# Stick-breaking attention: value products in groups of four units, in every other round, with a ring of ten turned tiles

## The reference

```python
def block(args):                       # one block of 128 queries
    z = q @ k.T * scale
    strict = key_pos < q_pos
    log_1mb = where(strict, log_sigmoid(-z), 0)
    after = reverse_cumsum(log_1mb) - log_1mb
    a = where(strict, exp(log_sigmoid(z) + after), 0)
    return a @ v
```

## Time and profile before

| | us |
|---|---|
| median of three runs | 2894.77 |
| the profiled execution, its own time | 2895.18 |
| its span | 2893.4 |
| attention stage, first scores to last output copy | 592.2 to 1050.5 |
| PE busy in the span | 2622.1 (91%) |
| DVE, ACT, POOL busy in the span | 1493.9, 1316.4, 629.1 |

### The profile page before, as it was taken

How to read it: one execution, slowest core, us unless ns; L and a number is a source line. 1 busy time by engine, 2 the same in 40 slices (tenths; PEclk the granted TensorE clock), 3 DMA queues, 4 the chain that set the end, 5 groups by cost and what they waited for, 6 DMA issues and landing times. The chain is left out here.

```text
span 2893.4 us, 46489 instructions
## 1 busy us (share of the span) xinstructions
PE 2622.1 (91%) x14633; PEld 2095.4 (72%) x14635; DVE 1493.9 (52%) x1975; ACT 1316.4 (45%) x2332; POOL 629.1 (22%) x697
## 2 busy tenths in 40 slices
PE   7999689979999979978999999949999999999991
PEld 6888578856667657757678888737777788888880
DVE  4222245578888862220433333265788855555643
ACT  4222233278989961100322222124777755555642
POOL 0000011157777730000000000031222211112223
PEclk9999899989999989989999999959999999999995
DMA  4333411242021022232312221143999966666856
GB/s 167 94 91 94 135 61 59 62 89 67 16 67 49 2 88 98 101 141 104 114 53 78 87 80 59 66 170 118 372 372 367 355 217 210 208 213 219 282 152 249
DMA packets 203097, 406.93 MB, mean 141 GB/s; under 512 B 26096, under 2 KB 67568, under 8 KB 202992
## 3 DMA queue, kind: packets, MB, share of 16 engines
q1 hardware_dynamic: 186576, 363.04, 36.1%
q0 software_dynamic: 13968, 33.59, 5.0%
q10 hardware_dynamic: 2448, 8.91, 0.8%
HBM read 339.39 MB, written 83.36 MB: 146 GB/s over the span
## 5 line engine op out<-in xcount | busy, mean ns | idle before, releaser
L746 POOL TENSOR_TENSOR stick_weight<-stick_weight,stick_left 128x512 f32<-128x512 f32 (+3 forms) x320 | 327.9, 1038 | 127.0 <-DVE stick_left L874 122.6
L1625 DVE TENSOR_TENSOR moe_w_lo<-moe_w_lo_raw,moe_w_hi (+1 forms) x256 | 297.7, 1220 | 57.6 <-ACT moe_w_hi L1621 51.8
L1621 ACT CAST moe_w_hi<-moe_w_lo_raw (+1 forms) x256 | 255.2, 1054 | 39.3 <-DMA moe_w_lo_raw<-in_w 29.3
L874 DVE TENSOR_TENSOR_SCAN stick_left<-stick_z_ps,stick_left,stick_any_row 128x512 f32<-128x512 f32 x192 | 240.3, 1276 | 35.4 <-ACT stick_z_ps L837 35.1
L835 ACT ACTIVATE stick_weight<-stick_z_ps 128x512 f32<-128x512 f32 (+3 forms) x320 | 173.6, 542 | 32.7 <-PE stick_z_ps L784 21.1
L797 PE MATMUL stick_t_ps<-all_ident,stick_weight 128*128 128x128 f32 x1088 | 165.2, 281 | 18.8 <-ACT stick_weight_t L844 9.2
L58 PE MATMUL exp_g_ps<-moe_w_hi,exp_x_hi 128*128 x376 | 154.7, 411 | 22.0 <-DVE moe_w_lo L1625 11.1
L837 ACT ACTIVATE stick_z_ps<-stick_z_ps 128x512 f32<-128x512 f32 (+3 forms) x320 | 165.7, 518 | 10.4
L797 PEld LDWEIGHTS stick_t_ps<-all_ident,stick_weight 128*128 128x128 f32 x1088 | 116.1, 141 | 69.7 <-issue 45.6
L58 PE MATMUL qkv_z_ps<-qkv_w_hi,qkv_h_hi 128*128 128x512 f32 x384 | 157.5, 410 | 4.0 <-DVE qkv_h_lo L238 4.0
L58 PE MATMUL exp_y_ps<-moe_w_hi,exp_h_hi 128*128 128x512 f32 x376 | 153.5, 408 | 2.3 <-DVE exp_h_lo L2054 2.3
(11 more groups left out here) (287 smaller groups left out, 5934.9 us busy)
## 6 DMA issues: line engine op xcount, KB each, us to landing
moe_w_lo_raw<-in_w SPq DMA_DIRECT2D x512, 256.0 KB
moe_w_lo_raw<-in_w SPq DMA_DIRECT2D x128, 512.0 KB
qkv_xs<-in_x SPq DMA_DIRECT2D x16, 512.0 KB, 4.7
qt_scratch<-qkv_q_t SPq DMA_DIRECT2D x16, 512.0 KB, 3.2
kt_scratch<-qkv_k_t SPq DMA_DIRECT2D x16, 512.0 KB, 3.5
gmlp_xs<-in_x SPq DMA_DIRECT2D x16, 512.0 KB, 3.7
mix_q<-qt_scratch SPq DMA_DIRECT2D x32, 256.0 KB
out_xs<-in_x SPq DMA_DIRECT2D x16, 512.0 KB, 3.4
```

The source lines that it names most:

```text
L746: nc.gpsimd.tensor_tensor(taken, taken, after, ALU.mult).then_inc(weight_done, 1)
L874: nc.vector.tensor_tensor_scan(row[:, c * BANK:c * BANK + keys][:, ::-1], back, any_row[:, 0:keys], start, ALU.mult, ALU.bypass).then_inc( ...
L1621: nc.scalar.copy(self.w13_hi[:, self.w13_at(e, i)], self.w13_raw[:, self.w13_at(e, i)]).then_inc(self.w13_cut, 1)
L1625: ops.tensor_tensor(self.w13_lo[:, self.w13_at(e, i)], self.w13_raw[:, self.w13_at(e, i)], as_f32(self.w13_hi[:, self.w13_at(e, i)]), ALU. ...
```

## The change

PE's round of even index (n a multiple of 4) now holds the value products of four units, n-8 to n-5; the other rounds hold none. The ring `weight_t` has ten slots where it had six. `put_out` stands two steps later in ACT's list (OUT_AT 9 where it was 7).

```diff
-    SLOTS, W_SLOTS, T_SLOTS, LEFTS = 4, 8, 6, 4
-    SCAN_AT, WEIGHT_AT, T_AT, AV_AT, OUT_AT = 1, 2, 4, 6, 7
+    SLOTS, W_SLOTS, T_SLOTS, LEFTS = 4, 8, 10, 4
+    SCAN_AT, WEIGHT_AT, T_AT, AV_AT, OUT_AT = 1, 2, 4, 8, 9
@@ in the list of PE @@
-                for n in range(0, n_units + AV_AT, 2):
+                for n in range(0, n_units + AV_AT - 3, 2):
                     if n < n_units:
                         scores(n)
                     if 0 <= n - T_AT < n_units:
                         turn(n - T_AT)
                         turn(n - T_AT + 1)
-                    if n >= AV_AT:
+                    if n >= AV_AT and n % 4 == 0:
                         gather_values(n - AV_AT)
+                        gather_values(n - AV_AT + 2)
```

## The result

The changed kernel takes 2939.96 us (median of four runs, 2938.71 to 2940.66), the kernel before 2893.73 beside it: 1.0161 times as long, 95% interval 1.0144 to 1.0179. The forecast was 2937, in a range of 2908 to 2954.

The account below looks back on a forecast made before the run. PE was taken to lead the attention stage, ACT and DVE close behind; switches -13.6, copy waits +61, scan waits -7.6 and output copies +2 gave +42 us on 2895.2: 2937 us, range 2908 to 2954.

Parts of the forecast that it names:

- The new wait: Even rounds' second turn on PE waits for a turned copy; 86 us against 24.9 before, growth +61 us.
- N: Time from ACT's start on an odd round's scores to the next round's second turn; 3.20 us for full units.
- The switches: Changes between kinds of matmul on PE, five instead of six in two rounds; 80 times 0.17 each, -13.6 us.
- Scan waits: Scores on PE waiting for scans; 7.6 us that longer rounds would cover, -7.6 us.
- The output copies: Second tile of grouped value products waits for the preceding output copy in seven places, 0.3 us each; +2 us.
- Faster by the switches alone: Rival: turned copies come in time and only the switches go; 2882 us, chance 0.07.
- No change, with ACT's own work as the limit: Rival: ACT's 5.71 us of work in two full rounds takes PE's saving; 2890 to 2900 us, chance 0.05.
- Clock: Rival: PE's clock falls as PE idles 1 us in 6.7; 2987 us, chance 0.04.

Follow-up runs that it names:

- e1: Changed kernel with the grouping undone (value products of two units every round), later value products and ring of ten kept; 2893.38 us, ratio 0.9996.
- e4: Changed kernel with the four units' value products between the even round's two turns instead of behind them; 2901.6 us, ratio 1.0026.
- e2: Changed kernel with the four units' value products in the odd rounds instead of the even ones; 2914.96 us, ratio 1.0072.
- e3: Changed kernel with the second unit's turned copy moved ahead of its sigmoids on ACT and of the first unit's scan on DVE; 2903.76 us, ratio 1.0032.
- e6: Changed kernel with the grouped value products ahead of both turns of the even round, two units later, ring of twelve; 2904.75 us, ratio 1.0041.
- e5: Kernel before the change, with the early turned copies of e3 on both ACT and DVE; 2887.61 us, ratio 0.9976.
- e7: Kernel before the change, with the early turned copies of e3 on ACT alone; 2893.15 us, ratio 0.9996.

## Why the prediction was right

**The new wait** held in place, cause and size. Cause: e1 shows that nothing but the grouping counts, e4 that the same grouped products cost 8 us, not 46, ahead of the turn, e2 that it depends on which round's time is emptied, e3 that shortening N alone brings back 36 us. Some cost stays with the grouping in every place tried: e3, e4 and e6 are still 8 to 11 us above the kernel before, and in each the scores wait for scans (25.9, 7.7 and 32.0 us listed on PE, where the kernel before has 0.3). Size: 87.4 - 1.3 = 86 us were forecast; the trace has 68.0 + 82 x 0.17 = 81.9. Growth 57 against 61.

**The switches.** 80 fewer at 0.17 each, -13.6, with the direct switch from turns to scores now seen at 0.17. The weight loader's gaps of 0.17 us agree with the rule of the Trainium skill (TensorEngine Tiling (Array Packing), Key Properties) that a change of tiling mode drains PE. By it alone the change was a gain; the saving was there, but the waits grew by four times as much, 57 against 13.6.

**Scan waits** were mis-sized. I took 7.6 us as waiting that longer rounds would cover; after, 7.1 us are still there. The pair of load rows above shows why: both gaps are 0.17, one is put down to DVE and one to nothing. The row of 7.6 us in 32 gaps holds 32 x 0.17 = 5.4 us of the switch itself, with the name of whatever semaphore came last. The PE row for scans, with 0.3 us in one wait, was the one to read; after, it has 1.4 us in 5. The term was -2 at most, and came out at nothing: the scores' gaps beyond the switch were 3 us and are 2.

**The output copies** were forecast at +2 and cost nothing here: no wait for L850 is listed on PE. The dependence was real, though, and appeared as 6.3 us in e3, once the turn no longer waited ahead of the products.

With the measured sizes: -13.6 + 57.0 = +43.4, against 43.3 in the stage. The forecast's +42 was near because two wrong terms (-7.6 and +2) and 4 us too much in the wait nearly cancel; that part was luck. So is the agreement to 0.1 us: by the weight loader's gaps ahead of turns (31 us before, 86 after) the wait grew by 55 and not 57, and the sum is good to some 2 us.

**The rivals.** Faster by the switches alone: the copies did not come in time; ACT had its pause, but its list order held the copy where it was. No change, with ACT's own work as the limit: ACT's busy time in 600 to 1050 us fell from 404.7 to 370.3 us, and its waits for scores grew. Clock: 1.00 in the whole of 600 to 1050 us, with waits up to 1.3 us. Where my expectations failed later (e3, e5, e6, e7, and e4 by little), it was mostly on the same point: I removed one wait and priced the next tight loop, scores to scans through four slots, too low.

## What to carry to other kernels

In an interleaved list, work on the leading engine is also the time in which other engines must deliver. Before moving a block, find for each wait behind it the chain that it covers (here scores, two sigmoids each, copy, second turn: 3.2 us against 3.3 us of cover), and compare block by block; a saving of 0.17 us of switching cannot pay for 1.03 us of cover. When a wait is removed, work out the next loop in the same way, with the queue order of every engine in it, before promising its whole price.

## What the runs showed of the hardware that was not expected

A gap of 0.17 us at a change of matmul kind is put down to another engine whenever a semaphore of that engine arrived last, though its wait cost nothing: the 160 score groups have 160 gaps both before (128 put down to nothing, 32 to DVE) and after (131 and 29), in all 0.19 us on average without the stage's first.

And idle time listed on PE is short of what a wait costs, since it counts from a matmul's modelled end. Ahead of a second turn the 1.21 us listed at 806.48 is a gap of 1.41 on the weight loader; I took 0.17 us for each such wait, so that 68.0 us listed were worth 81.9. Without that the stage's sum would be 36 us and not the 43 measured. Ahead of scores, where the switch takes 0.17 us in any case, hardly anything is missing: at 809.86 of e3's trace PE lists 0.68 us, the weight loader 0.91, of which 0.17 is the switch.

```profile
806.44 0.20 PEld L797 LDWEIGHTS stick_t_ps<-all_ident,stick_weight 128*128 128x128 f32 x2 [1.41 <-issue]
```

```profile
809.86 0.53 PEld L784 LDWEIGHTS stick_z_ps<-stick_k_other,mix_q 64*128 64x128 f32 x6 [0.91 <-DVE stick_left L878]
809.86 0.96 PE L784 MATMUL stick_z_ps<-stick_k_other,mix_q 64*128 64x512 f32 x6 [0.68 <-DVE stick_left L878]
```
